# Sums of activations made behind the norm's diagonal, and the norm's scale spread by two rounded products

## The reference, cut to what matters

```python
def rms_norm(x, g, eps=1e-6):
    y = x * lax.rsqrt(jnp.mean(x * x, axis=-1, keepdims=True) + eps)
    return y * g

def swiglu(h, w_gate, w_up, w_down):           # F = 2816
    return (jax.nn.silu(h @ w_gate) * (h @ w_up)) @ w_down

x = x + 0.5 * swiglu(rms_norm(x, ffn1_norm[l]), ...)   # l = 0, 1
...                                                    # convolutions, attention
x = x + 0.5 * swiglu(rms_norm(x, ffn2_norm[l]), ...)
...                                                    # second block, l = 0, 1
h = h + (silu(u @ w_gate[l]) * (u @ w_up[l])) @ w_down[l]    # u = rmsnorm(h, ffn_norm[l])
```

## Time and profile before

| | us |
|---|---|
| median of 3 runs | 3517.13 (3515.9 to 3517.22) |
| profiled execution | 3515.1 |
| its span, first to last instruction | 3513.3 |
| PE busy | 3449.7 (98%) |
| DVE busy | 2448.9 (70%) |
| ACT busy | 1406.2 (40%) |
| POOL busy | 928.6 (26%) |
| mean granted clock of PE | 0.991 |

### The profile page before, as it was taken

One profiled execution on the slowest core, in us unless ns is written; L12 is line 12 of the kernel. 1 busy time (PEld: TensorE's weight loads), 2 busy tenths in 40 slices (PEclk: granted clock), 3 DMA queues, 4 the chain that ended last, 5 costly groups with the idle time before them and its releaser, 6 DMA issues.

```text
span 3513.3 us, 51281 instructions
## 1 busy us (share of the span) xinstructions
PE 3449.7 (98%) x18454; PEld 2873.7 (82%) x18454; DVE 2448.9 (70%) x3362; ACT 1406.2 (40%) x2181; POOL 928.6 (26%) x631
## 2 busy tenths in 40 slices
PE   8999999999999999999999999999999999999998
PEld 7888786878888888878687888887788888878887
DVE  5677797568668857779746866855686584577756
ACT  4333365344234433336534423435433343443333
POOL 0112394022212311239402221320312140041213
PEclk9999999999999999999999999999999999999999
DMA  5332332323333333343232333322233332223331
GB/s 157 96 98 88 102 102 67 114 84 95 93 101 91 94 97 101 87 105 96 72 112 81 98 94 101 91 84 61 78 94 97 96 96 79 65 74 96 96 99 63
DMA packets 621281, 324.66 MB, mean 92 GB/s; under 512 B 13488, under 2 KB 616520, under 8 KB 621128
## 3 DMA queue, kind: packets, MB, share of 16 engines
q1 hardware_dynamic: 617096, 317.15, 31.2%
q10 hardware_dynamic: 4032, 5.51, 0.6%
HBM read 314.75 MB, written 2.10 MB: 90 GB/s over the span
## 4 chain that ended last, share of the span: by engine, by line
PE 85%; DVE 5%; issue 5%; POOL 2%; ACT 2%; DMA 0%; SPq 0%; POOLq 0%; DVEq 0%; ACTq 0%
PE bank L536 20%; PE bank L538 20%; PE bank L537 20%; PE bank L576 5%; PE bank L578 5%; PE bank L577 5%; PE bank L689 1%; POOL mem L2304 1%; PE bank L690 1%; PE bank L691 1%; DVE w_lo L1532 1%; DVE u_lo L1536 1%; PE bank L675 1%; PE bank L893 1%; PE bank L877 1%
## 5 line engine op out<-in xcount | busy, mean ns | idle before, releaser
L1073 ACT ACTIVATE w_hi<-raw 128x1024 fp32r<-128x1024 f32 x602 | 634.5, 1057 | 1219.8 <-PE bank L538 1206.6
L1532 DVE TENSOR_TENSOR w_lo<-raw,w_hi 128x1024 fp32r<-128x1024 f32 x602 | 831.7, 1384 | 236.9 <-ACT w_hi L1073 236.2
L536 PE MATMUL bank<-u_hi,w_hi 128*128 128x512 f32 x1920 | 770.2, 401 | 14.5 <-DVE u_lo L1536 12.5
L538 PE MATMUL bank<-u_hi,w_lo 128*128 128x512 f32 x1920 | 765.7, 399 | 0.0
L537 PE MATMUL bank<-u_lo,w_hi 128*128 128x512 f32 x1920 | 760.7, 396 | 0.0
L536 PE MATMUL bank<-h_hi,w_hi 128*128 128x512 f32 (+1 forms) x1568 | 607.5, 387 | 5.6 <-DVE h_lo L1536 4.8
L538 PE MATMUL bank<-h_hi,w_lo 128*128 128x512 f32 (+1 forms) x1568 | 607.2, 387 | 0.0
L537 PE MATMUL bank<-h_lo,w_hi 128*128 128x512 f32 (+1 forms) x1568 | 603.5, 385 | 0.0
L536 PEld LDWEIGHTS bank<-u_hi,w_hi 128*128 128x128 f32 x1920 | 362.8, 189 | 109.4 <-DVE u_lo L1536 17.6
L2271 POOL TENSOR_TENSOR mem<-raw 128x512 f32<-128x512 f32 x57 | 73.6, 1291 | 1389.6 <-DVE sum_lo L1586 698.6
L537 PEld LDWEIGHTS bank<-u_lo,w_hi 128*128 128x128 f32 x1920 | 362.7, 189 | 88.2 <-issue 2.4
(11 more groups left out here) (295 smaller groups left out, 5765.2 us busy)
## 6 DMA issues: line engine op xcount, KB each, us to landing
raw<-in_w_in SPq DMA_DIRECT2D x96, 512.0 KB, 3.8
raw<-in_ffn_w_gate SPq DMA_DIRECT2D x88, 512.0 KB, 3.8
raw<-in_ffn_w_up SPq DMA_DIRECT2D x88, 512.0 KB, 3.8
raw<-in_ffn_w_down SPq DMA_DIRECT2D x64, 512.0 KB, 3.8
raw<-in_w_gate SPq DMA_DIRECT2D x44, 512.0 KB, 3.8
raw<-in_w_up SPq DMA_DIRECT2D x44, 512.0 KB, 3.8
raw<-in_w_out SPq DMA_DIRECT2D x32, 512.0 KB, 4.2
raw<-in_xa_wkv SPq DMA_DIRECT2D x32, 512.0 KB, 4.0
```

The source lines that it names most:

```text
L536: mm(o, w_hi[:, s, w], rhs_hi[:, r], start=k == order[0], stop=False)
L538: ins = mm(o, w_lo[:, s, w], rhs_hi[:, r], start=False, stop=k == order[-1])
L1073: a(w_hi[:, p.slot, :], raw[:, p.slot, :], ACT.Copy).then_inc(rounded, 1)
L1532: tt(w_lo[:, p.slot, :], raw[:, p.slot, :], f32(w_hi[:, p.slot, :]), ALU.subtract).then_inc(split, 1)
```

## The change

1. `spread` makes two fp32r products, ones by `diag_hi` and ones by `diag_lo`, in place of one native float32 product. `split_diag` builds the diagonal as four rounded blocks and then, after a wait for them, four blocks of the rest; for q = 8 too. A rounded copy of the ones is made once at the start on DVE.
2. The four sums of activations are made whole, 128x1024 each (4 in place of 7 pieces). For q = 3, 4, 7, 9 and 11 they leave the loop over k = 0 to 7: DVE makes them right behind the diagonal, ahead of `gate` of chunk n; ACT rounds them after the tanh of chunk n, ahead of `h_hi`; DVE splits them behind `up` of chunk n+1. ACT still makes the scaled copies in the loop. For q = 0 they stay under the down projection, spread over one more chunk.
3. POOL waits for the diagonal (`stat_diag`) before the first weight sums of a fast part.
4. In the loop of fast pairs DVE makes `sum_lo` before the `w_lo` of that place, not after.

```diff
             def spread(q):
 
                 pe.wait_ge(stat_diag, q + 1)
-                mm(bank[7][:, :], ones, diag, start=True, stop=True).then_inc(stat_bc, 1)
+                mm(bank[7][:, :], ones_r[:, :], diag_hi[:, :], start=True, stop=False)
+                mm(bank[7][:, :], ones_r[:, :], diag_lo[:, :], start=False, stop=True).then_inc(stat_bc, 1)
...
+            def split_diag(values):
+
+                for t in range(NQ):
+                    ins = ts(diag_hi[:, t * P:(t + 1) * P], ident, values[:, t:t + 1], None, ALU.mult)
+                chain.done(v, ins)
+                for t in range(NQ):
+                    at = slice(t * P, (t + 1) * P)
+                    ins = stt(diag_lo[:, at], ident, values[:, t:t + 1], f32(diag_hi[:, at]), ALU.mult, ALU.subtract)
+                ins.then_inc(stat_diag, 1)
...
-                make_diag(j_inv if q == 8 else inv, diag, stat_diag)
+                split_diag(j_inv if q == 8 else inv)
...
+                if j == T1:
+                    v.wait_ge(t_src, KT * (FAST[q] + 1))
+                    ins = tt(b11, b11, b12, ALU.subtract)
+                elif j == T3:
+                    v.wait_ge(t_made, t0 + 1)
+                    ins = tt(b12, b22, b12, ALU.subtract)
+                elif j == T2:
+                    ins = tt(b22, b22, b11, ALU.add)
+                else:
+                    v.wait_ge(t_made, t0 + 3)
+                    ins = tt(b21, b22, b21, ALU.subtract)
+                ins.then_inc(t_made, 1)
...
                         if fast is not None:
-                            rest_of_summed(q, 1)
-                            rest_of_summed(q, 2)
+                            for j in T_ORDER:
+                                summed(q, j)
                         v.wait_ge(rstd_set, q + 1)
                         gate(At(n), None)
                         up(At(n + 1), 0, 0)
+                        if fast is not None:
+                            for j in T_ORDER:
+                                rest_of_summed(q, j)
                         rest_of_weights(At(n + 2))
...
                             gate(At(n, i), i * 2 + f0)
+                            rest_of_sums(m)
                             rest_of_weights(At(n, i))
-                            rest_of_sums(m)
...
                                     finish(q + 1, i * 4 + j, i * 4 + (gain + j))
-                                    source_sums(q + 1, i * 4 + j)
...
             def fast_sums(n, q):
 
                 fast = FAST[q]
+                pool.wait_ge(stat_diag, q + 1)
+
```

On ACT the rounding moves in the same way:

```diff
                         act.wait_ge(taken, n + RING + 1)
                         a(tanh_t, gate_t, ACT.Tanh, scale=0.5).then_inc(f_tanh, 1)
+                        if fast is not None:
+                            for j in T_ORDER:
+                                round_summed(q, j)
                         act.wait_ge(f_prod, F_TILES * f + 1)
                         a(tile(h_hi, 0), gate_t, ACT.Copy).then_inc(f_rounded, 1)
```

More of the change, by code:

```diff
@@ L99 @@
 T1, T3, T2, T4 = range(4)
-T_PARTS = [[(T1, slice(0, 4), 0)]] + [[(j, slice(2 * h, 2 * h + 2), 3 * h + j) for j in (T3, T2, T4)] for h in range(2)]
-T_COUNT = 7
+T_ORDER = (T1, T3, T2, T4)
+T_COUNT = 4
 def out_turns(eng, q):
@@ L220, in two_blocks @@
         w_hi, w_lo = sb("w_hi", [P, RING, CH], F32R), sb("w_lo", [P, RING, CH], F32R)
+        with ExitStack() as operands:
+            before_ones = operands.enter_context(nc.sbuf_tensor("before_ones", [P, C_ONE], F32))
+            ones_r = operands.enter_context(nc.sbuf_tensor("ones_r", [P, P], F32R))
         const = sb("const", [P, C_N])
@@ L228, in two_blocks @@
             t_hi, t_lo = (operands.enter_context(nc.sbuf_tensor(n, [P, 4, KT // 2, HS], F32R)) for n in ("t_hi", "t_lo"))
+            after_t = operands.enter_context(nc.sbuf_tensor("after_t", [P, 14084 - 10752], F32))
+            diag_hi = operands.enter_context(nc.sbuf_tensor("diag_hi", [P, S], F32R))
+            after_hi = operands.enter_context(nc.sbuf_tensor("after_hi", [P, S], F32))
+            diag_lo = operands.enter_context(nc.sbuf_tensor("diag_lo", [P, S], F32R))
         mem = sb("mem", [P, 16140])
@@ L269, in two_blocks @@
         ident = const[:, C_ID:C_ID + P]
-        ones = const[:, C_ONE:C_ONE + P]
-        one = const[:, C_ONE:C_ONE + 1]
+        ones, one = f32(ones_r[:, :]), f32(ones_r[:, 0:1])
         y_buf = [view(13572, S), view(14084, S)]
-        square, diag = y_buf
+        square = y_buf[0]
         last_square = view(15108, S)
@@ L1085, in step, with round_summed @@
                     round_weights(p)
-            def round_summed(q, part):
-                for j, ks, no in T_PARTS[part]:
-                    act.wait_ge(t_made, T_COUNT * FAST[q] + no + 1)
-                    a(t_hi[:, j, ks, :], t_sum[j][:, ks, :], ACT.Copy, scale=t_sign[j]).then_inc(t_rounded, 1)
+            def round_summed(q, j):
+                act.wait_ge(t_made, T_COUNT * FAST[q] + j + 1)
+                a(t_hi[:, j], t_sum[j], ACT.Copy, scale=t_sign[j]).then_inc(t_rounded, 1)
             def source(q, k, gain):
@@ L1137, in ffn @@
                             step(At(n))
-                        if fast is not None:
-                            round_summed(q, 2)
                         step(At(n + 1))
@@ L1168, in down @@
                             source(q + 1, k, gain + k)
-                        if not (q or g) and k in (3, 4, 5):
-                            round_summed(q, k - 3)
+                        if not (q or g) and k in (3, 4, 5, 6):
+                            round_summed(q, T_ORDER[k - 3])
                         if end and joint:
@@ L1586, in rest_of_sums, with summed, rest_of_summed @@
                 tt(sum_lo[:, :], w_sum, f32(sum_hi[:, :]), ALU.subtract).then_inc(s_split, 1)
-            def summed(q, part):
+            def summed(q, j):
                 t0 = T_COUNT * FAST[q]
                 b11, b12, b22, b21 = t_sum
-                if part == 0:
-                    v.wait_ge(t_src, KT * FAST[q] + 4)
-                    tt(b11, b11, b12, ALU.subtract).then_inc(t_made, 1)
-                    return
-                ks = slice(2 * part - 2, 2 * part)
-                b11, b12, b22, b21 = (b[:, ks, :] for b in t_sum)
-                v.wait_ge(t_src, KT * FAST[q] + 4 + 2 * part)
-                v.wait_ge(t_made, t0 + 1)
-                tt(b12, b22, b12, ALU.subtract).then_inc(t_made, 1)
-                tt(b22, b22, b11, ALU.add).then_inc(t_made, 1)
-                v.wait_ge(t_made, t0 + 3 * part)
-                tt(b21, b22, b21, ALU.subtract).then_inc(t_made, 1)
-            def rest_of_summed(q, part):
-                for j, ks, no in T_PARTS[part]:
-                    v.wait_ge(t_rounded, T_COUNT * FAST[q] + no + 1)
-                    stt(t_lo[:, j, ks, :], t_sum[j][:, ks, :], t_sign[j], f32(t_hi[:, j, ks, :]), ALU.mult, ALU.subtract)\
-                        .then_inc(t_split, 1)
-            def source_sums(q, k):
-                if q in FAST:
-                    if k == 3:
-                        summed(q, 0)
-                    if k == 5:
-                        rest_of_summed(q, 0)
-                        summed(q, 1)
-                    if k == 7:
-                        summed(q, 2)
+                if j == T1:
[10 more added lines that the diff above has]
+                ins.then_inc(t_made, 1)
+            def rest_of_summed(q, j):
+                v.wait_ge(t_rounded, T_COUNT * FAST[q] + j + 1)
+                stt(t_lo[:, j], t_sum[j], t_sign[j], f32(t_hi[:, j]), ALU.mult, ALU.subtract).then_inc(t_split, 1)
             def residual(p, k, factor):
@@ L1748, in plain_finish @@
                             finish(q, i * 4 + j, i * 4 + (gain + j))
-                            source_sums(q, i * 4 + j)
             def normalise(i, p, s_at):
@@ L1766, in _ @@
             rest_of_weights(At(0), 0)
+            nc.vector.tensor_copy(ones_r[:, :], const[:, C_ONE:C_ONE + P])
             for k in range(KT):
@@ L1776, in _ @@
             v.wait_ge(stat_inv, 1)
-            make_diag(inv, diag, stat_diag)
+            split_diag(inv)
             v.wait_ge(setup_in, 16 * 6)
```

10 lines of the change are left out of this document (4 added, 6 removed).

## The result

The changed kernel takes 3487.5 us (median of four, 3486.0 to 3488.6), the kernel before 3516.5 us (median of four, 3511.1 to 3517.2): ratio 0.992, 95% interval 0.9903 to 0.9938, 29.0 us or 0.8% faster. The forecast was 3495.4 us in a range of 3487 to 3509: the direction is right, and the time lies at the lower edge of the range, inside it by 0.5 us.

What follows compares the result with a forecast made beforehand. PE, busy 98% of the span, was taken as the bound. Excess at five norms 24.2 + spread 4.7 − squares 1.0 − new wait 6.25 = 21.7 us saved, from 3517.1 to 3495.4 us, range 3487 to 3509.

Steps and rivals of the forecast that it cites:

- What the sums in the loop cost: At norms q = 3, 4, 7, 9 and 11, excess over a quiet norm's 12.47 us: 24.2 us to win.
- POOL's squares: At q = 9 and 11 POOL's squares are what is late next; charged 0.5 us each, 1.0 together.
- rival (d): Stops at q = 9 and 11 stay, POOL's squares being as late as DVE was; 3504.4 us, chance 0.10.
- The spread: Two fp32r products replace the native one: 0.39 us saved, 12 times, 4.7 us; `diag_lo` costs nothing under 0.9 us of cover.
- The wait of POOL: At q = 3 and 7 POOL starts later, the diagonal is ready before the spread; 0.9 us each go.
- The new wait: First fast pair of five parts: PE waits 1.25 us for `sum_lo`, 6.25 us; S is the start of the spread.
- The swap: In the fast pairs, `sum_lo` ahead of `w_lo` spares 1.15 us, already counted in the chain to `sum_lo`.
- rival (b): At all five places a longer wait for `sum_lo` takes the clock along, costing 22.5 us; 3511.7 us, chance 0.17.
- The sum: Whole kernel: 24.2 + 4.7 − 1.0 − 6.25 = 21.7 us saved, giving a median of 3495.4 us.
- rival (a): At the five places no wait for `sum_lo`, as DVE makes up the 1.25 us; 28.0 saved, 3489 us, chance 0.18.

## Why the prediction held, point by point

**What the sums in the loop cost.** Forecast 24.2 us of excess at five norms; they take 12.33, 12.34, 12.34, 12.51 and 12.49 us now, 62.0 in all against five quiet norms of 12.47, so 24.2 + 0.3 = 24.5 us went. Right, and the kernel with the sums moved alone shows that this part carries it. At q = 11 the last `u_lo` ends at 3112.75 and its first product starts at 3112.96, without a wait: just in time, as worked out.

**POOL's squares.** I charged 1.0 us. The step from the last product on u to the sum of squares is 0.53 us at q = 11, and that norm is no longer than a quiet one to 0.02 us. At q = 3, 4 and 7 that step is 0.23 us, so the squares are late by at most 0.3 us at q = 9 and 11, 0.6 in all, and this is already in the lengths above. The term was 0.4 us too large, and rival (d) fell.

**The spread.** Forecast 0.39 us, measured 0.40 (1.09 to 0.70 at a quiet norm), 12 times, 4.8 us. But "so 0.9 us of cover is left and the cost is nothing" was wrong as a price of the part: `diag_lo` delays the sums by 1.1 us, and that made the new waits, so the part is worth 1.8 us net by the medians and nothing by the rows. It was in the sum all the same, since I started the chain at the end of the whole diagonal.

**The wait of POOL.** For the diagonal at q = 3 and 7 "whose 0.9 us each go": right in the kernel with that wait alone (1.4 us). As a value of the edit it was the worst of my numbers. With the sums moved and the diagonal doubled it keeps five stops of 3.0 to 3.3 us and their half clock away, 20 to 23 us. "Without the cover it would be 0.95 us, 11 times" priced a case that did not come: what takes the cover away is POOL, at five norms, and PE then stops for 3.0 to 3.3 us each time.

**The new wait.** Forecast by its own steps, counted from S, against the rows at q = 11 (S = 3120.55):

| step | forecast | measured |
|---|---|---|
| fourth sum done | S + 7.0 | S + 6.8 |
| gate done | 7.7 | 7.4 |
| last `t_hi` done | 12.3 | 11.9 |
| `h_lo` done | 13.6 | 13.1 |
| last `t_lo` done | 18.2 | 17.6 |
| `sum_lo` done | 27.0 | 26.3 |
| PE wants it | 25.75 | 25.75 |
| wait | 1.25 | 0.6 here, 1.0 at q = 3, 4, 7 |

Three sums are stretched, as forecast. PE's idle time by the rows is 0.42 to 0.84 us; the places lose 1.1, 1.1, 1.2 and 0.8 us, and q = 11 about as much as q = 9: 5.0 us where I had 6.25. The clock stayed full. The term was right in kind and 1.25 us too large. The rule cited there (the Trainium skill, SBUF — State Buffer, "SBUF: two separate sides") has a VectorE operation with two SBUF inputs and a GpSimd operation that reads SBUF shut each other out for a whole instruction. The trace agrees (2.20 to 2.31 us beside POOL, 1.22 alone), and the stop of 2.35 us worked out beside it for four stretched sums did not come, since POOL starts 0.48 us behind the first (3119.88 against 3119.40).

**The swap.** "Spares 1.15" was mis-sized: 2.1 us a place, because `w_lo` would wait for ACT besides. Without it, rival (b) comes true in the main: five stops of 2.5 to 2.9 us, half clock behind three of them, 3507.5 us, where I had put (b) at 3511.7. By the rows the five places then cost 21.8 us (16.8 and the 5.0 of after), where (b) had 22.5. The prediction let the length of the stop decide on the clock, kept at 1.3 us and lost at 2.7. The length alone does not settle it, since of three stops of 2.93 and 2.94 us one was followed by half clock and two were not. So (b) stood nearer than its chance said; one order of two instructions keeps it away.

**The sum.** 24.5 + 4.8 − 5.0 = 24.3 us by the rows, forecast 21.7, measured 25.5 to 29.0 (mean 27.4). Of the 7.9 us by which the first median lies under the forecast, 2.6 are in these terms, 0.6 in the median of before (3516.5, not 3517.1), and 4.7 in none. That the first median fell into the range at all is in part luck: its own terms, as measured, give 24.3 us, and the rest of the 29.0 is not in the prediction. Some 3 us of the mean gain have no place that I can name. The start and the two attention parts spread by up to 3.6 us each between profiles (second product behind the first spread at 32.6 to 36.2 us; norm 1 to 2 in 228.2 to 231.5; norm 5 to 6 in 228.2 to 231.7), in kernels whose code there is the same but for 0.4 us of spread, so they could hold it. In the attention parts the length goes with the time at half clock (6.8 us of it in the shortest, 13.7 or more in the longest). The start and these two parts together hold 23.9 us of half clock in the profile of before and 20.5, 30.7 and 20.5 us in the three of after, which shows no shift by the change; whether their mean shifts stays open. That the time fell on rival (a)'s 3489 us is no support for (a): its "no new wait" did not happen.

## All versions side by side

| kernel | us | ratio to before |
|---|---|---|
| spread alone | 3520.0 | 1.0013 |
| POOL's wait alone | 3514.3 | 0.9995 |
| sums moved (with swap) alone | 3496.7 | 0.9946 |
| sums moved, POOL's wait | 3492.0 | 0.9930 |
| sums moved, split spread | 3510.3 | 0.9984 |
| all of the change without the swap | 3507.5 | 0.9976 |
| the change | 3487.5, 3490.3, 3488.1 | 0.992, 0.9926, 0.9919 |
| the change, `t_hi` before the tanh | 3481.9, 3484.1 | 0.9904, 0.9911 |
| the change, POOL behind DVE's sums | 3484.0 | 0.9908 |
| the change with both moves | 3487.5 | 0.9917 |

The three parts alone add up to +4.3 − 1.4 − 19.1 = −16.2 us; together they give −27.4. The split spread is a loss of 4.3 us on before, a loss of 13.6 beside moved sums, and once POOL waits it shows as a gain of 1.8, which the intervals do not tell from nothing.

## What to carry to other kernels

Price each part of a change on top of the others, not on the kernel before: a guard that buys 1 us today can be what lets the next edit pay. Ask of every operation that is put behind another on VectorE which GpSimd work will lie beside it, and of two neighbours in a queue whose input comes first. Where ACT idles while it waits for a tanh's input, put the roundings that are ready there. And count a stop of some 3 us at up to twice its length: it may take the clock along.
